# Gathered rows as events of their own in the attention stages of a fused encoder step

## The reference, cut to what matters

```python
def layer(x, ...):
    proj = x @ w_in                                     # stage "project"
    o_a = stick_breaking_attend(sb_q, sb_k, sb_v)       # stage "stick"
    q, k_nope, v_mla = ...                              # stage "mla_project"
    o_b = mla_attend(q_nope, q_pe, k_nope, kpe, v_mla)  # stage "mla"
    merged = sigmoid(g_a) * (o_a @ w_oa) + sigmoid(g_b) * (o_b @ w_ob)
    h = layer_norm(ALPHA * x + merged @ w_out)          # stage "merge"
    y = layer_norm(ALPHA * h + peer(h))

def peer(h):                                            # block of 128 frames
    s = einsum(q(h), peer_sub_keys)                     # stage "scores"
    top_s, experts = top 16 of the pair sums of two top 16 lists
    g = softmax(top_s)
    act = gelu(einsum('thkd,td->thk', peer_u[experts], h))
    return einsum('thk,thkd->td', g * act, peer_v[experts])
```

## Time and profile before

| | us |
|---|---|
| median of 3 runs (lowest to highest) | 3553.65 (3553.0 to 3565.41) |
| the profiled execution, its own time | 3558.26 |
| its span, first to last instruction | 3556.5 |
| busy: PE, DVE, POOL, ACT | 3036.3, 2536.0, 1558.1, 1210.2 |
| `stick` and `mla` of group 1, about | 129 and 120 |
| `stick` and `mla` of group 2, about | 191 and 174 |
| `dense` | 1515 |

### The profile page before, as it was taken

How to read it: one execution, slowest core, us unless ns; L and a number is a source line. 1 busy time by engine, 2 the same in 40 slices (tenths; PEclk the granted TensorE clock), 3 DMA queues, 4 the chain that set the end, 5 groups by cost and what they waited for, 6 DMA issues and landing times. The chain is left out here.

```text
span 3556.5 us, 36144 instructions
## 1 busy us (share of the span) xinstructions
PE 3036.3 (85%) x10170; PEld 1717.7 (48%) x10170; DVE 2536.0 (71%) x5041; ACT 1210.2 (34%) x3181; POOL 1558.1 (44%) x1184
## 2 busy tenths in 40 slices
PE   8979989676889895775887898999989999989988
PEld 5755745344545453433654554444444444444443
DVE  0122069887786877877867678888888888788886
ACT  0241234665533435754552322222222222222221
POOL 0000025667662288888777533333333333333330
PEclk9989999785789997997688999999999999999999
DMA  4675589666799997576678999999999999999995
GB/s 144 217 254 177 190 311 394 207 181 202 222 321 359 338 341 218 145 202 181 183 248 301 406 404 399 399 405 396 404 378 412 400 407 398 397 393 407 400 408 204
DMA packets 375912, 1098.51 MB, mean 309 GB/s; under 512 B 91712, under 2 KB 210208, under 8 KB 289568
## 3 DMA queue, kind: packets, MB, share of 16 engines
q0 software_dynamic: 165072, 751.05, 56.6%
q1 hardware_dynamic: 176800, 303.85, 24.4%
q10 hardware_dynamic: 33840, 41.30, 3.3%
HBM read 1031.97 MB, written 63.02 MB: 308 GB/s over the span
## 5 line engine op out<-in xcount | busy, mean ns | idle before, releaser
L428 POOL DMA_INDIRECT expert_rows<-in_experts,picked_index x640 | 770.9, 1204 | 1271.1 <-DVE ff_sum L583 1157.1
L571 DVE SCALAR_TENSOR_TENSOR expert_rows<-expert_rows,h_tile 128x1024 f32<-128x1024 f32 x672 | 820.1, 1220 | 256.8 <-DMA expert_rows<-in_experts,picked_index 212.4
L583 DVE SCALAR_TENSOR_TENSOR ff_sum<-expert_rows,coefficients,ff_sum 128x1024 f32<-128x1024 f32 x672 | 860.8, 1281 | 92.2 <-ACT coefficients L534 75.9
L1786 PE MATMUL dense_act_ps<-dense_hT,key_columns 128*128 128x384 f32 x2048 | 724.7, 510 | 139.5 <-DMA key_columns<-in_key_columns 128.5
L451 POOL DMA_INDIRECT gates_by_expert<-dense_gate,gate_address x384 | 680.3, 1772 | 154.7 <-issue 129.2
L1775 PE MATMUL dense_out_ps<-dense_value_rows,dense_weights 128*128 128x512 f32 x1536 | 678.9, 592 | 0.5 <-DVE dense_weights L1854 0.5
L1786 PEld LDWEIGHTS dense_act_ps<-dense_hT,key_columns 128*128 128x128 f32 x2048 | 399.4, 198 | 482.8 <-DMA key_columns<-in_key_columns 196.2
L833 PE MATMUL proj_ps<-xT,w_in_block 128*128 128x384 f32 (+1 forms) x1392 | 424.1, 468 | 40.7 <-PEq L1595 16.5
L1775 PEld LDWEIGHTS dense_out_ps<-dense_value_rows,dense_weights 128*128 128x128 f32 x1536 | 291.8, 190 | 342.6 <-issue 309.7
L833 PEld LDWEIGHTS proj_ps<-xT,w_in_block 128*128 128x128 f32 x1392 | 268.3, 193 | 195.7 <-issue 37.9
L528 ACT ACTIVATE activated<-dots 128x1 f32<-128x1 f32 (+1 forms) x631 | 124.8, 198 | 638.5 <-DVE expert_rows L571 601.5
(11 more groups left out here) (186 smaller groups left out, 3144.8 us busy)
## 6 DMA issues: line engine op xcount, KB each, us to landing
key_columns<-in_key_columns SPq DMA_DIRECT2D x128, 512.0 KB, 11.6
dense_value_rows<-in_experts SPq DMA_DIRECT2D x128, 512.0 KB
gates_by_expert<-zeros POOLq DMA_DIRECT2D x12, 2048.0 KB, 21.9
wq_half<-in_peer_wq SPq DMA_DIRECT2D x48, 512.0 KB
dense_gates<-gates_by_expert SPq DMA_DIRECT2D x128, 192.0 KB
w_in_block<-in_w_in ACTq DMA_DIRECT2D x18, 1024.0 KB
w_in_block<-in_w_in SPq DMA_DIRECT2D x18, 1024.0 KB
w_out<-in_w_out SPq DMA_DIRECT2D x24, 512.0 KB, 7.5
```

The costliest lines, as they stand in the source:

```text
L428: pool.indirect_dma_start(to, None, self.a["experts"], bass.IndirectOffsetOnAxis(ap=index[:, k:k + 1], axis=0)).then_inc(self.got[p % self ...
L571: dve.scalar_tensor_tensor(place, place, 1.0, self.h[n % 2][:], ALU.mult, ALU.mult, accum_out=self.dots[:, s % TOPK:s % TOPK + 1]).then_in ...
L583: dve.scalar_tensor_tensor(total, self.ring[:, p % self.RING, D:2 * D], self.coef[:, y % TOPK:y % TOPK + 1], total, ALU.mult, ALU.add).the ...
L1786: mm = nc.tensor.matmul(up[it % 2][:, 0:W], keys[it % KB][:, k, :], hTd[:, k, :], start=(k == 0), stop=(k == KC - 1))
```

## The change

Every gathered row is now an event of its own, `("row", s)`, also in the four attention stages: DVE does one row step at an event, and POOL issues one row's fetch. ACT keeps a list `pending` and works on it when it has as many rows as the stage's batch, so the attentions still have two rows to one GELU (and one pair of table loads); what is left is done at the stage's end. As the attention lists get longer (74 to 83 and 61 to 70 events in group 1, 91 to 104 and 78 to 90 in group 2), rows, route stages and scatters fall at other places.

```diff
             while row < end or quantum < routed:
-                m = min(batch, end - row)
-                due = self.routed_before(row + m - 1) if row < end else 0
+                due = self.routed_before(row) if row < end else 0
...
-                    self.beside[block].append(("rows", row, m))
-                    row += m
+                    self.beside[block].append(("row", row))
+                    row += 1
...
     def dve(self, part):
         for e in self.upto("DVE", part):
-            if e[0] == "rows":
-                for s in range(e[1], e[1] + e[2]):
-                    self.dve_row(self.nc.vector, s)
+            if e[0] == "row":
+                self.dve_row(self.nc.vector, e[1])
...
     def act(self, part):
         for e in self.upto("ACT", self.last_part if part < 1 else 1):
-            if e[0] == "rows":
-                self.act_rows(self.nc.scalar, range(e[1], e[1] + e[2]))
+            if e[0] == "row":
+                self.pending.append(e[1])
+                if len(self.pending) == self.batch:
+                    self.act_pending()
...
+        if part >= 1:
+            self.act_pending()
         self.last_part = part
+
+    def act_pending(self):
+        if self.pending:
+            self.act_rows(self.nc.scalar, self.pending)
+            self.pending = []
...
-            for s in range(e[1], e[1] + e[2]) if e[0] == "rows" else ():
-                for p in self.fetch_at.get(s, []):
+            if e[0] == "row":
+                for p in self.fetch_at.get(e[1], []):
                     pool.wait_ge(self.used, p - self.RING + 1)
                     self.fetch(pool, p)
-                self.store(pool, s)
+                self.store(pool, e[1])
```

More of the change, by code:

```diff
@@ L301, in lay_out_loads @@
         k_of = {e: k for k, (_, _, e) in enumerate(points) if e[0] == "route"}
-        k_of |= {("row", s): k for k, (_, _, e) in enumerate(points) if e[0] == "rows" for s in range(e[1], e[1] + e[2])}
+        k_of |= {e: k for k, (_, _, e) in enumerate(points) if e[0] == "row"}
         key = lambda k: (points[k][0], points[k][1])
@@ L343, in begin @@
         self.events = self.beside.get(self.block, [])
-        self.at, self.last_part = {"DVE": 0, "ACT": 0}, 0
+        self.at, self.last_part, self.pending = {"DVE": 0, "ACT": 0}, 0, []
+        self.batch = next((batch for block, _, batch, _, _ in self.SHARES if block == self.block), 1)
         self.table = None
@@ L386, in pool @@
                 self.load_h(pool, n)
-            if e[0] == "rows" and e[1] == 0:
+            if e == ("row", 0):
                 for p in range(self.RING):
                     self.fetch(pool, p)
-            for s in range(e[1], e[1] + e[2]) if e[0] == "rows" else ():
-                for p in self.fetch_at.get(s, []):
+            if e[0] == "row":
+                for p in self.fetch_at.get(e[1], []):
                     pool.wait_ge(self.used, p - self.RING + 1)
                     self.fetch(pool, p)
-                self.store(pool, s)
+                self.store(pool, e[1])
             for r, k in self.scatter_at.get((self.block, i), []):
```

## The result

The changed kernel takes 3566.02 us (median of 20 runs, 3555.12 to 3572.44), the kernel before 3555.18 us beside it (20 runs, 3543.74 to 3565.41): the ratio is 1.003, 95% interval 1.002 to 1.0041. It is slower by 11 us, where 10 us faster was forecast; 3566 lies outside the range too. The profiled execution took 3563.1 us (span 3561.3).

The account below looks back on a forecast made before the run. No engine was full overall; DVE's row steps and waits were taken to bound the attentions, POOL group 2 from 1250 to 1638. +2.0 - 5.5 + 6.2 - 12 = -9.3 us from 3553.65 gave 3544, range 3529 to 3561.

Parts of the forecast that it names:

- stick, group 1: Stage's end gets longer by a table load and the last pair's GELU, partly hidden: +2.0 us, ends 0 and +3.3.
- nothing to lose where DVE never waited: stick of group 1: DVE waits only for the first softplus (5.5 us) and last output (3.4), never between; order can't shorten it.
- mla, group 1: 3 us off DVE's 7.8 of waits, 2.5 off the end behind the last maximum: -5.5 us, ends -10.3 and 0.
- stick and mla_project, group 2: POOL, full from 1250, gets 29 scatters instead of 26 ahead of the barrier at 1638: +6.2 us, ends 0 and +9.
- `stick` alone may end 2 us earlier or 3 later: Group 2: such a shift is hidden up to 1638 by the 11 us that DVE has to spare.
- My upper end, +9: stick and mla_project of group 2: +9 us if the order makes POOL wait once.
- POOL idle before 1638: Sign of being wrong: POOL, which never waits from 1250 to 1638 in the profile before, would stand idle there.
- mla, group 2: 9 us off DVE's waits for gathered rows, 3 off those for PE: -12 us, ends -22.9 and +3.
- doesn't bound this stage: mla of group 2: POOL has three scatters fewer and waited already (11.8 and 4.4 us), so it isn't the bound.
- Rival (c): mla of group 2: rows come no sooner, the fetch's queue place sets its time; whole -0.3 us, 3553; chance 0.17.
- ACT's 57.6 us: mla of group 2: ACT's waits ahead of a maximum, up to 15.5 us at once, would be cut by a third.
- Rival (a): POOL's three scatters stay and smoothing the attentions is worth nothing: +8.2 us, 3562; chance 0.14.

Follow-up runs that it names:

- e5: The changed kernel with the last two of the 18 rows of group 1's stick attention in one event again; 3558.78 us in one run.
- e12: The changed kernel, unchanged, profiled a second time; 3570.31 us in one run.
- e2: The changed kernel with single row events only in the two mla attentions, pairs in both stick attentions as before the change; 3549.47 us, ratio to before 0.9981.
- e8: The changed kernel with ACT taking each row by itself at once, not two at a time; 3571.26 us, ratio to before 1.0043.
- e1: The changed kernel with the scatters' credit in stick of group 2 divided by 104 instead of 90; 3551.49 us, ratio to before 0.9983.
- e4: The kernel before, pairs everywhere, with the scatters' credit in stick of group 2 divided by 78.75 instead of 90; 3573.75 us, ratio 1.005.
- e7: e1 with 45 scatters instead of 55 in mla of group 2; 3557.47 us, ratio to before 0.9996.
- e10: e1 with divisor 130 instead of 104 in stick of group 2, so 70 scatters instead of 55 in mla; 3554.29 us, ratio to before 0.9991.
- e11: The kernel before the change, unchanged, profiled a second time; 3553.48 us in one run.

## Why the prediction was wrong

*stick, group 1: +2.0 forecast, +5.2 and +4.8 measured.* The mechanism was seen, in the right rows, and sized too small. I took one load; what stands in the tail is a Gelu load, the pair, a wait for the index behind the last row step, and a load back. e5 takes out 2.8. Another 1.6 is lost ahead of the tail; that there was nothing to lose where DVE never waited was wrong, as it waits 9.5 us for ACT now, 5.5 before. The Trainium skill, page "ScalarE: Activation LUTs", section "What ACT_TABLE_LOAD costs", would add a drain to each load; in the tail after, the GELU starts 1.30 us behind its load's start again, so no drain shows.

*mla, group 1: -5.5 forecast, -5.3 measured* (-5.0 and -5.4 in e12 and e2). Right in the total, and in every kernel with single rows and ACT's pairs there; its parts were off both ways. From the first maximum to the last it took 107.9 us and takes 100.9, 7.0 less: 2.5 for the row step that went behind, and DVE's waits fell from 7.8 to 3.2, where I took 3 off. But behind the last maximum it takes 1.7 us more, as ACT now loads its table back between that maximum (at 932.79) and the last exponentials. That I had at nothing:

```profile
933.36 1.28 ACT L384 ACT_TABLE_LOAD   x1
934.66 0.79 ACT L1344 ACTIVATE probs<-score_ps,minus_max 128x640 f32<-128x640 f32 x1
```

That the two nearly cancel is luck. e8 adds that the gain hangs on putting off: without it the stage is at 122.2.

*stick and mla_project, group 2: +6.2 forecast, +17 measured.* This is the step that failed. That POOL decides was right, and so was the count of 29 scatters. What I held, "`stick` alone may end 2 us earlier or 3 later; between there and 1638 that is hidden", took POOL's list as a sum. I read off how many scatters there were and not where they stood between the rows. With the denser list DVE waited 18 us more for rows and scores, which made `stick` 13.6 us longer and not at most 3. No scatter was left waiting at the list's end, three rows stood there side by side, and POOL then stood 9.6 us for a place in the ring. The two stages end on POOL's list, so the 18 us don't come on top: 6.2 + 9.6 = 15.8 of the 17 (with the means over five profiles, 6.2 + 8.4 = 14.6 against 13). My upper end, +9 "if the order makes it wait once", had that wait at 2.8; my sign of being wrong, "POOL idle before 1638", came true. e1 and e4 show that the list is the cause, from both sides.

*mla, group 2: -12 forecast, about -4 measured.* The waits for rows were to go because each fetch has longer to arrive. They were 10.1 us and are 5.7 after, with 51 scatters; in e2, with all 54, they are 9.0. First after, then e2:

```profile
DVE expert_rows L580 <- DMA expert_rows<-in_experts,picked_index: 5.7, 2, 3.8
```

```profile
DVE expert_rows L584 <- DMA expert_rows<-in_experts,picked_index: 9.0, 5, 2.5
```

That POOL "doesn't bound this stage" is the premise that failed. Rival (c) fits better: POOL starts with a queue, so a fetch's place in it sets its time, and e7 and e10 show the stage and the waits for rows move with the scatters in it. Nor did the waits ahead of maxima shrink: ACT's 57.6 us became 40.2, and what it lost there stands at the next line, 38.6 where it was 24.6.

```profile
ACT L384 <- DVE minus_max L1379: 40.2, 9, 15.5
ACT probs L1344 <- DVE minus_max L1379: 38.6, 12, 6.9
```

How much of the 4 us is the split is open: single rows gave 166.8 to 172.3 here, pairs 170.7 to 174.0, and two profiles of one kernel are 2 us apart.

*The whole.* -9.3 forecast, +10.8 by the medians. The four parts add up to +12.8 in the profiles, 22 us from the forecast: 11 are the scatters' order and POOL's stop, 8 the `mla` of group 2, 3 the tail. (The two profiled executions are only 4.8 us apart; the other stages were together some 8 us shorter after, while in e12 they were some 5 us longer than in e11.) Rival (a) gave 3562 and was nearest, though for another reason: the split was worth 5 us in one stage, and it lost 17 in another, for a number that no longer fitted. I gave slower by over 0.5% 0.05 and no change 0.75; the ratio of 1.003 is within that bound, and within it the sign was wrong.

## What to carry to other kernels

Where one list of events paces several things, a finer grain for one of them changes the rate of the others: look for every divisor, cap and credit that counts events, and compare the engines' order piece by piece, not its totals. On an engine that is full, ask of each instruction that others wait for how much stands ahead of it, and whether the last piece of the list leaves the engine something to do until the next release. A change that helps in one stage and harms in the next is worth splitting by stage, since here the stages added up for the most part.

## What the runs showed of the hardware

How well stages repeat: in `stick` of group 1, each of the 24 softplus came at the same time from the stage's start within 0.2 us in five profiles with the order of before, and within 0.4 in seven with the changed order, though the whole execution varies by 20 us from run to run. What varies is mostly elsewhere, as in `scores` of group 1, 112.2 to 119.2 us with the same order there. So one profile tells 3 us in a stage that repeats, where one whole run can't. How far POOL's records lag: 11 and 12 indirect DMAs behind the barriers at the ends of `project` and `mla_project` of group 2, in all 14 profiles. And a scatter has two prices: it takes 2.07 us of POOL, but taken out of `stick` of group 2 it saved 0.1 us there and 0.5 in `mla_project` behind it, and put into `mla` it cost 0.7, by what else waited for POOL.
